# Four more modulation blocks beside the first layer's heads on VectorE, and TensorE's two turns cut at units 50 and 59

## The reference, cut to what matters

```python
for l in range(DEPTH):
    sh_l, sc_l, g_l = jnp.split(jax.nn.silu(c) @ w_mod[l] + b_mod[l], 3, axis=-1)
    sh_c, sc_c, g_c = jnp.split(jax.nn.silu(c_ctx) @ w_mod[l] + b_mod[l], 3, axis=-1)
    hl = xl * (1.0 + sc_l[:, None, :]) + sh_l[:, None, :]
    hc = xc * (1.0 + sc_c) + sh_c
    parts_l = jnp.split(hl @ w_in[l], SPLIT_POINTS, axis=-1)
    ...   # rope, differential attention over both, convolution, pooling, w_out, layernorm
```

## Time and profile before

| | |
|---|---|
| median of 3 runs | 2875.14 us (2873.31 to 2875.14) |
| profiled execution, its own time | 2876.09 us |
| its span, first to last instruction | 2874.4 us |
| TensorE busy | 2846.0 us, 99% |
| VectorE busy | 1876.2 us, 65% |
| ScalarE busy | 1328.1 us, 46% |
| mean granted TensorE clock | 0.998 |

### The profile page before, as it was taken

One profiled execution on the slowest core, in us unless ns is written; L12 is line 12 of the kernel. 1 busy time (PEld: TensorE's weight loads), 2 busy tenths in 40 slices (PEclk: granted clock), 3 DMA queues, 4 the chain that ended last, 5 costly groups with the idle time before them and its releaser, 6 DMA issues.

```text
span 2874.4 us, 42472 instructions
## 1 busy us (share of the span) xinstructions
PE 2846.0 (99%) x15570; PEld 2384.3 (83%) x15570; DVE 1876.2 (65%) x3394; ACT 1328.1 (46%) x2044; POOL 112.5 (4%) x179
## 2 busy tenths in 40 slices
PE   8999999999999999999999999999999999999998
PEld 6778787777788788888888888888888888888887
DVE  3368686764577636666886666667876556565566
ACT  2343333323332534544556555556656445354445
POOL 0000000101000001111000100000000000000000
PEclk9999999999999999999999999999999999999999
DMA  9954444443365334344445544444555555555555
GB/s 377 361 192 182 164 166 177 162 171 152 152 237 206 117 105 157 136 147 148 171 162 191 191 174 178 171 180 171 183 189 202 191 186 197 190 181 199 188 192 190
DMA packets 78220, 530.66 MB, mean 185 GB/s; under 512 B 9416, under 2 KB 11728, under 8 KB 15472
## 3 DMA queue, kind: packets, MB, share of 16 engines
q1 hardware_dynamic: 73872, 515.95, 49.1%
q0 software_dynamic: 3328, 10.63, 1.1%
q10 hardware_dynamic: 864, 1.95, 0.2%
HBM read 526.37 MB, written 2.12 MB: 184 GB/s over the span
## 4 chain that ended last, share of the span: by engine, by line
PE 96%; DVE 1%; DMA 1%; ACT 1%; issue 1%; POOL 0%; POOLq 0%; ACTq 0%; DVEq 0%; SPq 0%
PE bank L2015 28%; PE bank L2018 14%; PE bank L2005 9%; PE bank L2007 9%; PE bank L2006 9%; PE bank L2425 4%; PE bank L2426 4%; PE bank L2424 4%; PE bank L2051 2%; PE bank L2052 2%; PE bank L2053 2%; PE bank L2234 1%; DMA raw<-stream 1%; PE bank L2193 1%; PE bank L2064 1%; PE bank L2074 1%
## 5 line engine op out<-in xcount | busy, mean ns | idle before, releaser
L1182 DVE TENSOR_TENSOR w_lo<-raw,w_hi 128x1024 fp32r<-128x1024 f32 x784 | 947.2, 1224 | 439.6 <-ACT w_hi L670 437.0
L670 ACT ACTIVATE w_hi<-raw 128x1024 fp32r<-128x1024 f32 x784 | 823.4, 1056 | 651.0 <-DMA raw<-stream 214.8
L2005 PE MATMUL bank<-x,w_hi 128*128 128x512 f32 x1120 | 442.8, 395 | 3.0 <-issue 1.8
L2007 PE MATMUL bank<-x,w_lo 128*128 128x512 f32 x1120 | 436.2, 389 | 0.0
L2006 PE MATMUL bank<-x,w_hi 128*128 128x512 f32 x1120 | 436.1, 389 | 0.0
L683 ACT ACTIVATE z<-bank 128x512 f32<-128x512 f32 x256 | 153.3, 599 | 472.3 <-PE bank L2018 298.2
L2015 PE MATMUL bank<-xs,w_hi 128*128 128x512 f32 x1184 | 303.9, 397 | 0.0
L2005 PEld LDWEIGHTS bank<-x,w_hi 128*128 128x128 f32 x1120 | 210.2, 188 | 70.1 <-issue 26.8
L2015 PE MATMUL bank<-mlp_x,w_hi 128*128 128x512 f32 x1024 | 257.1, 393 | 0.0
L2007 PEld LDWEIGHTS bank<-x,w_lo 128*128 128x128 f32 x1120 | 210.2, 188 | 44.6
L2015 PEld LDWEIGHTS bank<-xs,w_hi 128*128 128x128 f32 x1184 | 213.8, 189 | 40.1 <-DVE xs L1292 1.1
(11 more groups left out here) (353 smaller groups left out, 3590.4 us busy)
## 6 DMA issues: line engine op xcount, KB each, us to landing
raw<-stream SPq DMA_DIRECT2D x488, 1024.0 KB, 4.8
res<-tokens POOLq DMA_DIRECT2D x8, 512.0 KB, 8.9
work<-tokens POOLq DMA_DIRECT2D x16, 256.0 KB, 3.1
res<-cond_rows SPq DMA_DIRECT2D x8, 256.0 KB, 4.2
out<-res SPq DMA_DIRECT2D x8, 256.0 KB, 2.4
gain_sb<-final_gain ACTq DMA_DIRECT2D x1, 1024.0 KB, 6.0
table_sb<-tables ACTq DMA_DIRECT2D x1, 640.0 KB, 3.5
pool_sb<-pool_w POOLq DMA_DIRECT2D x8, 64.0 KB, 2.2
```

What stands on the lines that cost most here:

```text
L670: own.inc(act.activation(w_hi[:, 2 * unit.parity + g, :], raw[:, unit.slot, g * HALF:(g + 1) * HALF], ACT.Copy), hi_done, 2 * unit.number ...
L1182: own.inc(dve.tensor_tensor(w_lo[:, n, :], raw[:, unit.slot, g * HALF:(g + 1) * HALF], w_hi[:, n, :].bitcast(F32), ALU.subtract), lo_done, ...
L2005: pe.matmul(bank[:, :], hi, tile(k)[:, 0, :], start=k == 0, stop=False)
L2007: ins = pe.matmul(bank[:, :], lo, tile(k)[:, 0, :], start=False, stop=k == KT - 1)
```

## The change

`TURN_ENDS` becomes 50 and 59, and blocks 14, 25, 37 and 49 leave `BESIDE_PE`, so that they fall to `BESIDE_DVE`: 28 blocks on VectorE, 20 on TensorE. The first turn still has twelve blocks (12, 13, 16, 21, 26, 28, 33, 38, 40, 41, 45, 50), the second eight (52 to 59). The columns move with them: the second layer's modulation from column block 52 instead of 56 is laid out for VectorE (`SUMMED`), and `ROWS` goes from 6 to 7. At a turn's end ScalarE asks for the blocks of VectorE numbered below the unit's number plus two, instead of below the unit's number.

```diff
-SUMMED = 56
+SUMMED = 52
-TURN_ENDS = [40, 59]
-BESIDE_PE = [12, 13, 14, 16, 21, 25, 26, 28, 33, 37, 38, 40, 41, 45, 49, 50, *range(52, 60)]
+BESIDE_PE = [12, 13, 16, 21, 26, 28, 33, 38, 40, 41, 45, 50, *range(52, 60)]
+TURN_ENDS = [50, 59]
 ...
 def mods_before(turn):
-    return 2 * turn if turn < KT else 32 + 4 * BESIDE * (turn - KT)
+    return 2 * turn if turn < KT else min(32 + 4 * BESIDE * (turn - KT), SUMMED)
 ...
                     if l == 0 and unit.fixed in TURN_ENDS:
-                        act.wait_ge(share_used, sum(n < unit.fixed for n in BESIDE_DVE))
+                        act.wait_ge(share_used, sum(n < unit.fixed + 2 for n in BESIDE_DVE))
                         take_mod(KT + TURN_ENDS.index(unit.fixed), 1, 1)
 ...
             def later_modulation(turn):
-                modulation(turn, 1, [(mods_before(turn), 0, BESIDE, 0, 4)])
+                first = mods_before(turn)
+                modulation(turn, 1, [(first, 0, (mods_before(turn + 1) - first) // 4, 0, 4)])
```

## The result

The changed kernel takes 2884.6 us (median of 9 runs, 2879.6 to 2885.0) against 2874.8 of the kernel before in the same series; the ratio is 1.0029, 95% interval 1.0021 to 1.0037. So it is slower, by 6.0 to 10.6 us. (One of the nine runs of before, at 3128.7, was disturbed and is left out of the ratio.) The median lies 0.4 above the upper end of the forecast range, 2884.2; the forecast was reckoned from a before of 2875.1, and 1.0029 times that is 2883.5. The profiled execution spans 2883.3 us against 2874.4, 8.8 more before rounding.

The account below looks back on a forecast made before the run. The prediction took TensorE, 99% busy, as the bound; -0.84 for blocks, +5.6 for the pause and +2.0 for the clock made +6.8 us, a median of 2881.9 us, range 2878.5 to 2884.2.

Parts of the forecast that it names:

- The bound: Units 12 to 59, first layer: TensorE waits only 1.8 us, so work removed gains time and added waits cost in full.
- Four blocks for 0.84 us: Seams before units 14, 25, 37, 49: each block leaving TensorE gives 0.21 us, four of them 0.84.
- VectorE's four blocks for nothing: During units 13, 24, 36, 48: blocks of about 6.1 us fit VectorE's 7.7 to 7.1 us free, costing nothing.
- The pause of 5.6 us: Middle of unit 50: TensorE idles 5.6 us until VectorE finishes block 51 and ScalarE copies the turn.
- The clock, 2.0 us: After unit 50's pause: the granted clock falls to 0.50 and products at half speed lose 2.0 us.
- Rival A: Unit 50: the pause comes but the clock holds or costs little, +4.8 us, 2879.9; chance 0.23.
- B: Unit 50: the wait is hidden, leaving the gain of -0.84 us, 2874.3; chance 0.07.
- C: Unit 50 and the four seams: the wait is hidden and blocks pay in full, -4.8 us, 2870.4; chance 0.02.
- D: Units 48 to 50: VectorE is late, the pause grows to as much as 11.7 us, up to +13, 2888; chance 0.06.

Follow-up runs that it names:

- the fourth run: The kernel before, its 24 blocks on each engine kept, with turns of sixteen and eight, the first ending at unit 50 behind the wait for block 51: 2884.1 us.
- the fifth: The changed kernel with the first turn's collect moved within unit 50, after 36 of its 48 products instead of 24: 2878.4 us, ratio 1.0008.
- the third run: The changed kernel with the pause kept but filled by eleven matmuls of 32 x 256 on TensorE ahead of unit 50's collect: 2879.9 us, ratio 1.0015.
- the second run: The changed kernel with the first turn copied and collected one unit later, in the middle of unit 51: 2876.2 us, ratio 1.0005.

## Why the prediction was right, and where it was off

**The bound.** Right: the only waits that TensorE gained are the ones that the prediction names, and units 51 to 75 give nothing back of what they cost.

**Four blocks for 0.84 us.** Right: 0.83 in the changed kernel and with the pause undone. The seam before unit 14, with block 14 gone, in the timelines of TensorE and, last, ScalarE:

```profile
176.19 0.39 PE L2008 MATMUL bank<-x,w_lo 128*128 128x512 f32 x1
177.31 0.47 PE L2006 MATMUL bank<-x,w_hi 128*128 128x512 f32 x1 [0.73 <-DVE w_lo L1182]
177.61 0.40 PE L2007 MATMUL bank<-x,w_hi 128*128 128x512 f32 x1
...
176.61 0.60 ACT L683 ACTIVATE z<-bank 128x512 f32<-128x512 f32 x1 [2.61 <-PE bank L2008]
```

From last to second product 1.42 us, against 1.65 with the block and the 1.44 that the prediction read at another seam. TensorE now shows an idle 0.73 where the block stood, and starts 0.10 us behind the copy's end (177.21). The Trainium skill (Perfetto Trace Analysis, Identifying the Most-Contended Engine) says to optimize the engine with the highest occupancy first. By its busy share of 99% that is TensorE here, and yet a block taken off it gave back 1.17 us at the seam of block 41 and only 0.2 at the plain ones; that relief pays in full was the prediction's own inference, and it does not hold at every seam.

**VectorE's four blocks for nothing.** Right. Its windows for units 13 and 48 of the changed kernel, where the earlier trace rows had 4.41 and 4.94 busy:

```profile
165.39:177.31 11.92, 9.96 (x27) 1.00 0.55 192
609.16:621.03 11.87, 10.51 (x25) 1.00 0.57 204
```

1.36 us are left in the tighter one, and no wait on TensorE follows.

**The pause of 5.6 us.** Right in place, cause and releaser. Reckoned as the prediction did, from where the next product would have started, it is 5.47 us (5.31 of it idle in the trace). The step that was too large is TensorE's waking, 0.14 us behind the copy and not the 0.28 read at the earlier trace rows; ScalarE's start, 0.04 us behind the block's end, was left out.

**The clock, 2.0 us.** The mechanism was right and the term was too small: 2.9 in the changed kernel, 2.3 in the fourth run, 3.0 in the fifth. The prediction let the low stretch begin 3 to 4 us after the last product, from the earlier trace rows, so that a good part of its 6.83 us would pass inside the pause. In the changed kernel it began 4.5 us after it, only 0.8 us before TensorE woke, and 6.05 of the 6.83 us lay over matmuls. Nor did the stretch end sooner because dense products returned at once, for which the prediction had taken a little off: it lasted 6.83 us in all three. Two falls were too few to say when in a pause a third would come. The fifth run shows the other side of that: a fall 2.1 us after the last product, in a pause of 2.6. "Longer than both" was no test of whether the clock falls. The Trainium skill (TensorE: Matmul & The Clock Gate, HAM oscillation — how this bites in real kernels) warns that gaps between groups of matmuls throttle the clock and the next group starts cold; the traces agree, with 0.50 behind all three bare pauses of 2.6 us and more in the heads.

Rival A, the pause without the clock, was priced at 2879.9; the third run, which is just that, took 2879.9, 5.1 above before where A said 4.8. B and C asked for the wait to be hidden, D for VectorE to be late; neither is in the trace. The sum in the heads was +6.8 by the prediction, and +7.5 in the profiled pair: -0.1 by the pause, +0.9 by the clock. The further 1.4 us by which the two profiled executions differ lie in stretches that the change doesn't touch, and vary between executions.

## What to carry to other kernels

Price work taken off the busiest engine at the seam where it stood: from the last instruction before it to the second behind, with and without, at a like place of the same trace. If it lay over a wait, only the difference comes back (0.2 of 1.2 us here). When a hand-over moves, follow the whole chain at the new place, engine by engine: here a buffer that was shared with nobody late at unit 40 was shared with a block that ends 10.3 us into unit 50, and one unit later ScalarE was still at work on its exponentials.

## What the runs showed of the hardware that was not expected

In the one execution profiled, a pause of 2.6 us in the middle of dense products was followed by 6.83 us at a granted clock of 0.50 (1.2 GHz), and cost more by the clock, 3.0 us, than by itself, 2.75. One of 0.9 us in the second run, and the seams of 0.3 and 0.7, were not followed by a low stretch. With thin matmuls of 32 x 256 through a pause of 5.3 us the clock stayed at 1.00. Where within a pause the clock falls varied: 2.1, 3.2 and 4.5 us after the last product in three executions.
